# Running one token tile through all layers before the other, with the first tile's expert gather beside the second tile's layers

## The chip, the cores and the metric

The kernel runs on one core of a Trainium2 chip. The metric is the device time of one execution in microseconds, as the median of several runs. All data are float32.

## What is computed

The input `x` has 256 tokens of 1024 channels. Two layers (depth 2) of a mixed block come first, then one block of another kind, then a final RMS norm. Cut to what matters:

```
for l in range(2):                       # layers 0 and 1
    h = x @ w_in[l]                      # 1024 -> 6048, split into ten parts
    y_hg  = hgrn2(q, f, i)               # gated recurrence, 8 heads, causal
    y_mla = latent attention, 8 heads, causal
    y_mem = attention of every token over 256 memory tokens (mem @ w_k, mem @ w_v)
    y = concat(y_hg*silu(g), y_mla*silu(g), y_mem*silu(g)) @ w_out[l]
    x = layernorm(alpha * x + y)
mod = silu(c) @ w_ada + b_ada            # 6 rows of 1024: shifts, scales, gates
h = rmsnorm(x) * (1 + sc1) + sh1
x = x + g1 * (concat(dilated causal attention(h), causal pooling(h)) @ w_out_2)
h2 = rmsnorm(x) * (1 + sc2) + sh2
# experts: 8 heads; per head the top 16 of 128 + 128 sub-keys, then the top 16 of 256 sums
x = x + g2 * sum over 8 heads * 16 picks of  gate * gelu(u[e] . h2) * v[e]
out = rmsnorm(x)
```

Every token picks 128 of 16384 experts. An expert is a row of 2048 numbers (u and v side by side, 8 KB). A token depends on earlier tokens only (and on the memory tokens), never on later ones.

## The kernel before, in words

The tokens stand in two tiles of 128 (`TT = 2`). In layers 0 and 1 every product takes both tiles at once: `channel_major` (L671) multiplies a 128x128 block of weights with 256 token columns, `token_major` (L686) and `output_product` (L707) take 512 weight columns against 128 tokens. Weights are streamed once, as 48 units of mostly 2 MB, into a ring of three slots; SP's queue issues them (`weights`, L497) when the unit three places earlier has been used. The 24 pieces of `w_ada` (1 MB each) go into one buffer, are multiplied by silu(c) on GpSimd (L596 to L599), and are summed over partitions by TensorE in the tasks `AD`.

The order of work on each engine is written out by hand: `PE_ORDER`, `ACT_ORDER`, `DVE_ORDER` for the two layers and a last list each for the third block (L58 to L83). An engine takes its tasks in exactly this order and waits on semaphores where a task's input isn't there. `L01` to `L18` are the levels of the recurrence (products L811, blend L1631), `S`, `P`, `Y` the three steps of an attention batch, `HO`, `HN` the readout and its norm, `LN` the LayerNorm. In the third block `Xt`/`Xu`, `Zt`/`Zu` turn the first and second tile, `K0` to `K3` are the products of the expert queries (L965), `E` the scores against the sub-keys (L975), `R` the search for the top 16 (`route`), `XP` the expert numbers (`experts_of`, L1797 to L1817), `GT` the gates.

The gather begins when the first head's expert numbers are there. GpSimd issues one indirect DMA per pick (L632): partition p receives the row of token p's expert, 128 rows of 8 KB, 1 MB in all. 15 buffers of the earlier layers, freed one by one, take turns as slots (`NEW_SLOTS`, `PICK`). For each pick DVE forms the dot of the row's first half with h2 (L1847), ScalarE takes Gelu and gate (L1313, L1315) and scales an identity matrix by it (L1321), and TensorE multiplies this 128x128 diagonal with the row's second half, 512 columns at a time, into two PSUM banks over 128 picks (L1095). Then the slot may be filled again. First come all 128 picks of the first tile, then those of the second.

## Time and profile before

| | |
|---|---|
| median of 3 runs | 1444.62 us (1444.59 to 1448.75) |
| the profiled execution | 1450.41 us, span 1448.6 us |
| TensorE busy (matmuls) | 1296.5 us, 89% |
| weight loads of TensorE | 803.2 us, 55% |
| DVE busy | 814.1 us, 56% |
| ScalarE busy | 412.2 us, 28% |
| GpSimd busy | 643.4 us, 44% |
| DMA | 407.78 MB, mean 281 GB/s |

The span is the time from the first to the last instruction of the profiled execution. Busy times are for the whole span and average over stages with different limits; matmul ends are modelled, and matmuls overlap in the array, so the time from one start to the next tells more than a mean duration. Each float32 matmul of the program shows as two records. In the lists of waits the name after the arrow is what the engine waited for last.

### The profile page before, as it was taken

To read this page: it belongs to the slowest core of one execution; us is meant where nothing else is said; L and a number is where in the kernel's file an instruction comes from. 1 tells how busy PE (TensorE), PEld (TensorE's weight loads), DVE (VectorE), ACT (ScalarE), POOL (GpSimd) and SP (SyncE) were. 2 spreads that over 40 slices of the span, in tenths; PEclk is the share of its full clock that TensorE was granted. 3 is DMA by queue.
4 is the path that set the end of the run, shared out by engine and by line. 5 is a ranking of instruction groups with operands and counts; after the bars stand their busy time and mean duration, and the time that the engine had idled before them with its cause. 6 is when DMAs were issued, how large, how long until landed. Compare 5 with 4: busy or idle time off the path is not lost.

```text
span 1448.6 us, 16824 instructions
## 1 busy us (share of the span) xinstructions
PE 1296.5 (89%) x5960; PEld 803.2 (55%) x5960; DVE 814.1 (56%) x1681; ACT 412.2 (28%) x1032; POOL 643.4 (44%) x643
## 2 busy tenths in 40 slices
PE   9999999999999999999998989967977787777786
PEld 8877686547877686548656546523333333333332
DVE  0776277331566287432238765789797554544455
ACT  0532333201333333211223332322313232122123
POOL 0556667422546666513102544454544454444450
PEclk9999999999999999999998999988988899999999
DMA  9544234444444344445355999999999999999994
GB/s 374 190 161 175 117 155 186 161 175 175 180 161 175 117 174 188 171 167 200 132 217 209 407 420 392 420 420 419 421 419 420 420 420 420 421 420 420 420 420 203
DMA packets 53597, 407.78 MB, mean 281 GB/s; under 512 B 6133, under 2 KB 8586, under 8 KB 10890
## 3 DMA queue, kind: packets, MB, share of 16 engines
q0 software_dynamic: 36864, 268.45, 45.0%
q1 hardware_dynamic: 15562, 137.21, 24.2%
q10 hardware_dynamic: 1088, 1.05, 0.4%
q8 instruction: 47, 0.77, 0.2%
q14 instruction: 36, 0.29, 0.1%
HBM read 404.56 MB, written 1.07 MB: 280 GB/s over the span
## 4 chain that ended last, share of the span: by engine, by line
PE 29%; DMA 24%; DVE 7%; issue 4%; POOL 3%; ACT 2%; ACTq 0%; POOLq 0%; DVEq 0%
DMA ring<-in_peer_uv,vM 12%; PE bank L1095 9%; PE pj L671 6%; PE pj L707 6%; DMA yT<-in_peer_uv,vM 5%; PE pj L686 3%; DMA qvE<-in_peer_uv,vM 3%; PE pj L965 2%; DMA hv<-in_peer_uv,vM 2%; DMA more_rows<-in_peer_uv,vM 1%; DMA qM<-in_peer_uv,vM 1%; POOL more_rows L598 1%; DVE tri L1847 1%; POOL mod_part L599 1%; DVE big L1847 1%
## 5 line engine op out<-in xcount | busy, mean ns | idle before, releaser
L671 PE MATMUL pj<-xT,ring 128*128 128x256 f32 (+2 forms) x1536 | 326.5, 373 | 2.2 <-ACTq L1143 1.7
L671 PEld LDWEIGHTS pj<-xT,ring 128*128 128x128 f32 (+1 forms) x1536 | 279.3, 190 | 43.2 <-issue 3.6
L598 POOL TENSOR_SCALAR more_rows<-more_rows,lbt 128x256 f32<-128x256 f32 x168 | 172.0, 1024 | 16.4
L632 POOL DMA_INDIRECT ring<-in_peer_uv,vM x101 | 121.5, 1203 | 125.8 <-PE bank L1095 115.0
L596 POOL TENSOR_SCALAR mod_part<-more_rows,lbt 128x256 f32<-128x256 f32 x24 | 26.3, 1096 | 265.5 <-issue 122.0
L707 PE MATMUL pj<-ring,yT 128*128 128x512 f32 x320 | 141.9, 600 | 0.0
L599 POOL TENSOR_TENSOR mod_part<-mod_part,more_rows 128x256 f32<-128x256 f32 x168 | 128.0, 762 | 14.0
L1313 ACT ACTIVATE rope<-vM 128x4 f32<-128x4 f32 (+3 forms) x84 | 17.1, 204 | 408.5 <-DVE big L1847 326.1
L1095 PE MATMUL bank<-ring,tri 128*128 128x512 f32 x204 | 101.4, 638 | 20.9 <-ACT tri L1321 20.9
L1095 PE MATMUL bank<-ring,causal 128*128 128x512 f32 x200 | 99.6, 637 | 19.5 <-ACT causal L1321 19.5
L707 PEld LDWEIGHTS pj<-ring,yT 128*128 128x128 f32 x320 | 60.7, 193 | 72.0 <-issue 72.0
L1847 DVE SCALAR_TENSOR_TENSOR big<-ring,memT 128x1024 f32<-128x1024 f32 x51 | 62.9, 1233 | 48.9 <-DMA ring<-in_peer_uv,vM 48.7
L1847 DVE SCALAR_TENSOR_TENSOR tri<-ring,memT 128x1024 f32<-128x1024 f32 x50 | 61.2, 1224 | 48.6 <-DMA ring<-in_peer_uv,vM 48.5
L1095 PEld LDWEIGHTS bank<-ring,tri 128*128 128x128 f32 x204 | 41.3, 206 | 76.4 <-issue 48.9
L1095 PEld LDWEIGHTS bank<-ring,causal 128*128 128x128 f32 x200 | 39.6, 203 | 72.9 <-issue 45.5
L632 POOL DMA_INDIRECT more_rows<-in_peer_uv,vM x20 | 22.6, 1128 | 122.5 <-DVE vM L1817 79.4
L686 PE MATMUL pj<-ring,xT 128*128 128x512 f32 x160 | 70.5, 595 | 0.0
L1315 ACT ACTIVATE rope<-rope,rstd 128x1 f32<-128x1 f32 x256 | 56.6, 284 | 2.8
L1631 DVE COPY_PREDICATED tri<-level_mask,bank 128x512 f32<-128x512 uint8 x56 | 41.0, 731 | 16.9 <-PE bank L811 14.4
L632 POOL DMA_INDIRECT yT<-in_peer_uv,vM x28 | 31.4, 1121 | 41.0 <-PE bank L1095 39.2
L686 PEld LDWEIGHTS pj<-ring,xT 128*128 128x128 f32 x160 | 29.8, 190 | 34.7 <-issue 34.4
L965 PEld LDWEIGHTS pj<-xT,ring 128*128 128x128 f32 x320 | 44.1, 202 | 5.8 <-issue 4.3
(368 smaller groups left out, 2124.3 us busy)
## 6 DMA issues: line engine op xcount, KB each, us to landing
ring<-in_units SPq DMA_DIRECT2D x44, 2048.0 KB, 9.5
more_rows<-in_w_ada SPq DMA_DIRECT2D x24, 1024.0 KB, 4.8
ring<-in_units SPq DMA_DIRECT2D x2, 1536.0 KB, 6.3
ring<-in_peer_uv,vM POOLq DMA_INDIRECT x101, 23.3
memT<-in_mem SPq DMA_DIRECT2D x1, 1024.0 KB, 5.2
ring<-in_units SPq DMA_DIRECT2D x2, 512.0 KB, 6.6
ring<-in_units SPq DMA_DIRECT2D x1, 1024.0 KB, 9.1
xT<-in_x_turned SPq DMA_DIRECT2D x1, 1024.0 KB, 10.8
```

The lines of the kernel that those rows point to most:

```text
L596: do(g.tensor_scalar(part, mod_w[:, 0, :], silu_c[:, 0:1], None, ALU.mult))
L598: do(g.tensor_scalar(mod_w[:, c, :], mod_w[:, c, :], silu_c[:, c:c + 1], None, ALU.mult))
L599: do(g.tensor_tensor(part, part, mod_w[:, c, :], ALU.add), "mod_partial" if c == DC - 1 else None)
L632: pool.indirect_dma_start(row_slot[k], None, d["peer_uv_2"], bass.IndirectOffsetOnAxis(ap=expert[:, t, j:j + 1], axis=0))\
L671: ins = nc.tensor.matmul(pj[s][0:n, 2 * m + first:2 * m + stop], ring[:, slot, at:at + n], act[:, c, first:stop], start=(c == 0), stop=(c ...
L686: ins = nc.tensor.matmul(pj[s][:, t * COLS:(t + 1) * COLS], act[:, c, t * P:(t + 1) * P], w[:, c, :], start=(c == 0), stop=(c == DC - 1))
L707: ins = nc.tensor.matmul(pj[t][:, n * 512:(n + 1) * 512], yT[:, 4 * j + c, t * P:(t + 1) * P], w[:, c, n * 512:(n + 1) * 512], start=(firs ...
L965: ins = nc.tensor.matmul(pj[s][:, 2 * m * P + first:2 * m * P + stop], w[c][:, m * P:(m + 1) * P], xT[:, c, first:stop], start=(c == 0), s ...
L1095: ins = nc.tensor.matmul(bank[2 * (1 - t) + half][:, :], diag[n % N_DIAG], row_slot[PICK[n][0]][:, c0:c0 + COLS], start=(j == 0), stop=(j ...
L1315: a.activation(weights_of[:, n0 + k:n0 + k + 1], acts[:, n0 + k:n0 + k + 1], ACT.Copy, scale=gate[:, t, j + k:j + k + 1]).then_inc(sem("ro ...
L1631: do(v.copy_predicated(dst, mask, B), *bank_free(key))
L1847: v.scalar_tensor_tensor(out=junk[0 if one else n % 2], in0=row_slot[k][:, 0:D_MODEL], scalar=1.0, in1=normed[:, t, :], op0=ALU.mult, op1= ...
```

## The change

The work is done one tile at a time: stages (layer, tile) in the order (0,0), (1,0), (2,0), (0,1), (1,1), (2,1). The parts:

- Every product of the layers now has 128 token columns (or 128 tokens against 256 weight columns in `token_major`). The weights are cut into pieces of 1 MB (half a unit) in a ring of three 1 MB slots, and each piece is loaded once per tile: 184 loads, 96 for the first tile (8 of them for the memory keys and values, made only once) and 88 for the second.
- What the second tile needs of the first (keys, values, the recurrence's values and cross decays, memory keys and values) is stored to DRAM from each layer and loaded back before the second tile's same layer (`ST`, `LS`: five parts, 2.9 MB per layer each way). For the third block the first tile's keys, values and pooling input stay in SBUF (`kvu`).
- The pooling's running sums on GpSimd become products with window matrices (`MX`) on TensorE.
- The four engines' orders, SP's too, are one list each over all stages. In them the first tile's routing and picks (`D`, `W`: dots, weights and sums of one pair) stand between the second tile's tasks: W0 to W8 before the second tile's first output product, W9 to W33 before that of layer 1, W63 at the end of its expert queries.
- Modulation weights have a ring of four buffers instead of one; all 24 pieces are done within the first tile's stages.
- The first tile's gather has six slots of its own (`slots`), a seventh from pick 64 and an eighth from pick 107; the second tile's gets six more.
- Picks come in pairs. One indirect DMA still moves 128 rows: those of 64 tokens for two picks. h2 is kept in a matching arrangement (`HR`), four copies per part lay out expert numbers and gates (`paired`), and the scaled diagonal has 128 rows and 64 columns (`twice` is the identity folded in two). A pair takes four matmuls with 64 output partitions and 512 columns, as against four with 128 output partitions for two picks before.
- A dot is written in place over the row's first half.

The core of the diff:

```diff
+STAGES = [(0, 0), (1, 0), (2, 0), (0, 1), (1, 1), (2, 1)]
+RING, MOD_RING, FIRST_SLOTS = 3, 4, 6
+AFTER_ROUTING = (0, 1)
+NEW_SLOTS = {0: [0, 1, 2, 3, 4, 5], 64: [6], 107: [10], 136: [7, 8, 9, 11], 140: [12], 167: [13]}
...
-    for n in range(ROWS):
+    for n in range(TT * PICKS):
         if n in NEW_SLOTS:
-            free = list(NEW_SLOTS[n][1]) + free
+            free = list(NEW_SLOTS[n]) + free
         k = free.pop(0)
         out.append((k, last.get(k), sum(1 for q in out if q[0] == k)))
         last[k] = n
-        free.append(k)
+        if n % 2:
+            free += [out[n - 1][0], k]
     return out
...
+        state = [nc.dram_tensor(f"state{l}", (P, 5 * D_MODEL + COLS), f32).ap() for l in range(DEPTH)]
+
+        def state_parts(l):
+
+            y = state[l]
+            return ((kM[:, :, 0:P], y[:, 0:D_MODEL].rearrange("p (h t) -> p h t", t=P)),
+                    (hv[:, 0, :], y[:, D_MODEL:2 * D_MODEL]), (wide(cross[:, :, :]), y[:, 2 * D_MODEL:3 * D_MODEL]),
+                    (kvE[:, :, :].rearrange("p a n -> p (a n)"), y[:, 3 * D_MODEL:5 * D_MODEL]),
+                    (vM[:, 0, :], y[:, 5 * D_MODEL:5 * D_MODEL + COLS]))
 
...
+            def piece(n):
+
+                token = LOADS[n]
                 if n >= RING:
-                    sp.wait_ge(sem("unit_done"), n - RING + 1)
-                slot, first, width = n % RING, 0, UP_W if STREAM[n][1] == "UP" else DC * COLS
+                    old = LOADS[n - RING]
+                    task = old[3:]
+                    if task == "UQ":
+                        bank_filled(sp, old + ":1")
+                    elif task == "UK":
+                        bank_filled(sp, old[:3] + "UV")
+                    elif task[0] == "O":
+                        after(sp, "out_done", old)
+                    elif task[2:] == "a":
+                        after(sp, "half_done", old)
+                    else:
...
+                elif task == "ST":
+
+                    for k in ("I0", "I1", "J0", "J1", "J2", "J3"):
+                        after(sp, k + "_ready", s + k)
+                    after(sp, "uk_ready", s + "UK")
+                    after(sp, "uv_ready", s + "UV")
+                    sp.wait_ge(sem("kr_spread"), 32 * COUNT["kr_sent"][s + "Cr"])
+                    after(sp, "lvl_ready", s + "Db8")
+                    for held, kept in state_parts(l):
+                        sp.dma_start(kept, held).then_inc(sem(f"state_store{l}"), 16)
+                elif task == "LS":
+
+                    for k in range(DEPTH):
+                        sp.wait_ge(sem(f"state_store{k}"), 16 * STATE)
+                    done = "01." if l else "10."
+                    for k in (f"S{batches(1 if l else 0) - 1}", f"Y{batches(1 if l else 0) - 1}", "R1"):
+                        bank_filled(sp, done + k)
+                    for held, kept in state_parts(l):
+                        load(held, kept, "state_load")
+                elif task == "SB":
+
...
+            starts = {t * PICKS + first * TOPK: f"2{t}.XP{part}" for t in range(TT) for part, (first, last) in enumerate(EXPERT_PARTS)}
+            for n in range(TT * PICKS):
+                t, q, c = n // PICKS, n % PICKS // 2, n % 2
+                k, earlier, _ = PICK[n]
                 if n in starts:
-                    pool.wait_ge(sem("experts"), starts[n])
-                if previous is not None:
-                    pool.wait_ge(sem("rows_used"), previous + 1)
...
+                if n == 0:
+                    bank_filled(pool, "MT")
+                    pool.wait_ge(sem("mod_store"), 16)
+                    unit_done(pool, "10.J3")
+                if earlier is not None:
+                    pool.wait_ge(sem("rows_used"), earlier // 2 + 1)
+                elif k == KM_SLOT:
+                    bank_filled(pool, f"11.S{n_mla(1) - 1}")
+                elif RING_SLOT <= k < QK_SLOT:
+                    unit_done(pool, "21.H3")
+                elif k == QK_SLOT:
+                    bank_filled(pool, "21.S3")
+                    after(pool, "sm_ready", "21.S3")
+                elif k == QK_SLOT + 1:
+                    unit_done(pool, "21.H3")
+                elif k == QK_SLOT + 2:
+                    bank_filled(pool, "21.E3")
+                elif k == QK_SLOT + 3:
+                    after(pool, "routed", "21.RT7")
                 pool.indirect_dma_start(row_slot[k], None, d["peer_uv_2"],
-                                        bass.IndirectOffsetOnAxis(ap=expert[:, t, j:j + 1], axis=0))\
+                                        bass.IndirectOffsetOnAxis(ap=expert[t][:, q, c:c + 1], axis=0))\
                     .then_inc(sem(f"row_load{k}"), 16)
...
+                    elif token[0] == "W":
+                        p = int(token[1:])
+                        tile, q = p // PAIRS, p % PAIRS
+                        sums = acc if tile == 0 else pj
+                        if q == 0:
+                            if tile == 0:
+                                pe.wait_ge(sem("acc_free"), EARLY_USES)
+                            else:
+                                for s in range(2):
+                                    pe.wait_ge(sem(f"pj_free{s}"), WIDE_USES[s])
+                        pe.wait_ge(sem("diag_ready"), 2 * p + 2)
                         for half in range(2):
-                            c0 = D_MODEL + half * COLS
-                            ins = nc.tensor.matmul(bank[2 * (1 - t) + half][:, :], diag[n % N_DIAG],
-                                                   row_slot[PICK[n][0]][:, c0:c0 + COLS],
-                                                   start=(j == 0), stop=(j == PICKS - 1))
-                            if j == PICKS - 1 and half == 0:
+                            for c in range(2):
+                                n = 2 * p + c
+                                c0 = D_MODEL + half * COLS
+                                ins = nc.tensor.matmul(sums[64 * c:64 * c + 64, half * COLS:(half + 1) * COLS],
+                                                       diag[:, n % N_DIAG, :], row_slot[PICK[n][0]][:, c0:c0 + COLS],
+                                                       start=(q == 0), stop=(q == PAIRS - 1))
+                            if q == PAIRS - 1 and half == 0:
                                 last(ins, "half_summed")
                         last(ins, "rows_used")
...
+            def expert_weights(p):
+
+                tile, q = p // PAIRS, p % PAIRS
+                part = next(n for n, (a0, a1) in enumerate(EXPERT_PARTS) if a0 <= 2 * q // TOPK < a1)
+                after(act, "gate_ready", f"2{tile}.GT{part}")
+                act.wait_ge(sem("dot_done"), 2 * p + 2)
+                do(a.activation(acts[tile][:, q, :], dots[tile][:, q, :], ACT.Gelu))
+                for c in range(2):
+                    a.activation(weights_of[tile][:, q, c:c + 1], acts[tile][:, q, c:c + 1], ACT.Copy,
+                                 scale=gate[tile][:, q, c:c + 1]).then_inc(sem("row_weight"), 1)
+                if 2 * p >= N_DIAG:
+                    act.wait_ge(sem("rows_used"), p - N_DIAG // 2 + 1)
+                for c in range(2):
+                    act.wait_ge(sem("row_weight"), 2 * p + c + 1)
+                    a.activation(diag[:, (2 * p + c) % N_DIAG, :], twice[:, :], ACT.Copy, scale=weights_of[tile][:, q, c:c + 1])\
+                        .then_inc(sem("diag_ready"), 1)
...
+            def paired(dst, src, first, end, signal=None):
+
+                q0, q1 = first * TOPK // 2, end * TOPK // 2
+                for c in range(2):
+                    for a0 in range(2):
+                        done = c == a0 == 1
+                        do(v.tensor_copy(dst[64 * a0:64 * a0 + 64, q0:q1, c], src[64 * c:64 * c + 64, a0:(end - first) * TOPK:2]),
+                           *((signal,) if done and signal else ()), **({} if done else {"behind": 1}))
...
+                        p = int(token[1:])
+                        tile, q = p // PAIRS, p % PAIRS
+                        if q == 0:
+                            after(dve, "h2_ready", f"2{tile}.HR")
+                        for c in range(2):
+                            k, _, use = PICK[2 * p + c]
+                            dve.wait_ge(sem(f"row_load{k}"), 16 * (use + 1))
+                            row = row_slot[k][:, 0:D_MODEL]
+                            v.scalar_tensor_tensor(out=row, in0=row, scalar=1.0, in1=h2_of[tile][:, c, :], op0=ALU.mult, op1=ALU.mult,
+                                                   accum_out=dots[tile][:, q, c:c + 1]).then_inc(sem("dot_done"), 1)
...
+                elif task == "HR":
+                    bank_filled(dve, s + "Z:1")
+                    if t:
+                        bank_filled(dve, f"11.Y{batches(1) - 1}")
+                    do(v.tensor_tensor(normed, normed, row_scale2, ALU.mult))
+                    do(v.tensor_tensor(h2_of[t][0:64, 0, :], normed[0:64, :], row_shift2[0:64, :], ALU.add))
+                    do(v.tensor_tensor(h2_of[t][64:P, 1, :], normed[64:P, :], row_shift2[64:P, :], ALU.add), "h2_own")
```

## Rows read from the trace of the kernel before

**Rows 1.** The page: 40 equal slices of the span, and the gather's queue.
```profile
GB/s 374 190 161 175 117 155 186 161 175 175 180 161 175 117 174 188 171 167 200 132 217 209 407 420 392 420 420 419 421 419 420 420 420 420 421 420 420 420 420 203
...
q0 software_dynamic: 36864, 268.45, 45.0%
```

**Rows 2.** Windows: us, busy time by engine (instructions), TensorE clock, DMA share, GB/s.
```profile
0.00:741.00 741.00, 719.92 (x4403) 523.38 (x4404) 360.07 (x591) 216.78 (x354) 342.41 (x387) 0.99 0.47 180
...
741.00:850.00 109.00, 97.41 (x465) 65.59 (x464) 75.54 (x229) 35.84 (x99) 36.74 (x30) 0.94 0.72 289
...
850.00:1436.00 586.00, 475.18 (x1089) 212.91 (x1087) 371.41 (x849) 155.18 (x569) 264.19 (x227) 0.92 1.00 413
...
1436.00:1448.60 12.60, 3.97 (x8) 1.35 (x8) 7.10 (x14) 4.45 (x12) 0.00 (x0) 0.80 0.11 42
```

**Rows 3.** Timeline, 760 to 772 us: first head's routing, its expert numbers, first gather.
```profile
762.59 0.49 DVE L1760 MAX8 cT<-sm 128x8 f32<-128x128 f32 x2 [6.92 <-ACTq L1421]
...
767.23 0.18 DVE L1797 CAST cT<-kE 128x32 f32<-128x32 uint32 x1
...
770.19 0.17 DVE L1817 CAST vM<-vM 128x16 uint32<-128x16 f32 x1
...
771.29 1.17 POOL L632 DMA_INDIRECT more_rows<-in_peer_uv,vM  x1 [79.39 <-DVE vM L1817]
```

**Rows 4.** Chain of waits in order of time: start us, us, what, records.
```profile
502.11 20.83 PE pj L671 x96
...
546.54 13.93 PE pj L686 x32
...
757.25 3.59 PE pj L965 x32
...
871.19 6.87 PE bank L1095 x16
```

**Rows 5.** Groups by line and form, TensorE: the memory products.
```profile
L671 PE MATMUL pj<-memT,ring 128*128 128x256 f32 x128 | 28.2, 380 | 0.2 <-DMA ring<-in_units 0.2
...
L686 PE MATMUL pj<-ring,memT 128*128 128x512 f32 x64 | 27.8, 592 | 0.0
```

**Rows 6.** Timeline, DVE, from LayerNorm's scaling to the last block's turned rows.
```profile
654.26 1.28 DVE L1734 SCALAR_TENSOR_TENSOR pT<-x,stat,big 128x1024 f32<-128x1024 f32 x1
...
663.42 1.75 DVE L1550 TENSOR_SCALAR xT<-bank,modc 128x128 f32<-128x128 f32 x4 [2.03 <-PE bank L644]
```

**Rows 7.** Groups by line, GpSimd: the modulation's products and sums.
```profile
L598 POOL TENSOR_SCALAR more_rows<-more_rows,lbt 128x256 f32<-128x256 f32 x168 | 172.0, 1024 | 16.4
...
L599 POOL TENSOR_TENSOR mod_part<-mod_part,more_rows 128x256 f32<-128x256 f32 x168 | 128.0, 762 | 14.0
```

**Rows 8.** Groups by line, DVE: blend, level step, dot.
```profile
L1631 DVE COPY_PREDICATED tri<-level_mask,bank 128x512 f32<-128x512 uint8 x56 | 41.0, 731 | 16.9 <-PE bank L811 14.4
...
L1602 DVE TENSOR_TENSOR big<-b 128x512 f32<-128x512 f32 x28 | 25.6, 916 | 1.0
...
L1847 DVE SCALAR_TENSOR_TENSOR tri<-ring,memT 128x1024 f32<-128x1024 f32 x50 | 61.2, 1224 | 48.6 <-DMA ring<-in_peer_uv,vM 48.5
```

**Rows 9.** Groups by line, ScalarE: table loads at the Gelu.
```profile
L1313 ACT ACT_TABLE_LOAD x8 | 10.3, 1283 | 20.0 <-DVE big L1847 11.2 <-DVE tri L1847 8.6 <-ACT yT L1394 0.2
```

**Rows 10.** Timeline, TensorE: attention values in 64 columns, and the product after them.
```profile
105.80 0.66 PE L791 MATMUL bank<-pT,vM 128*64 128x128 f32 x8
...
106.39 0.92 PE L671 MATMUL pj<-xT,ring 128*128 128x256 f32 x3
```

**Rows 11.** The page's DMA issues: count, KB each, median us to landing.
```profile
ring<-in_units SPq DMA_DIRECT2D x44, 2048.0 KB, 9.5
...
more_rows<-in_w_ada SPq DMA_DIRECT2D x24, 1024.0 KB, 4.8
```

**Rows 12.** DMA issues, 800 to 850 us.
```profile
ring<-in_units SPq DMA_DIRECT2D x1, 2048.0 KB, 12.0
```

**Rows 13.** DMA issues, 850 to 900 us.
```profile
ring<-in_peer_uv,vM POOLq DMA_INDIRECT x8, 9.5
```

2668 lines of the change are left out of this document (1278 added, 1390 removed).

## The prediction

> **What bounds the kernel now.** I read the windows first, then the chain of waits, then the DMA rows. The kernel has two halves with different limits. Up to 741 us TensorE is busy 720 us while the DMA engines move only 180 GB/s; from 850 to 1436 us the DMA share is 1.00 at 413 GB/s and no engine is full [rows 1, 2]. The second half is the gather: 268.45 MB on the software queue [rows 1], 256 indirect loads of 1.05 MB, 128 for each token tile. The first is issued at 771.3 us, because the first expert numbers are ready only at 770.4 us [rows 3]. The slices hold 420 GB/s, so a picked row costs 2.5 us; 12.6 us of finish follow the last landing [rows 2]. So the time is: TensorE time to the first expert, plus bytes after it over 420 GB/s, plus the finish. The profiled execution took 1450.4 us for its span of 1448.6, and is 5.8 us above the median of 1444.6.
>
> **The part before the first gather.** The change halves the tokens of each product. Does a narrow product cost half? Matmuls are recorded twice each; 96 records with 256 columns took 20.8 us (217 ns), 32 with 128 columns 3.6 us (112 ns), 32 and 16 with 512 columns 13.9 and 6.9 us (435, 429 ns) [rows 4]. Cost goes by columns, so nothing is lost. Of the 720 us, the memory products take 27.5 each for the two forms (128 records at 215 ns, 64 at 430) [rows 5]; they are made once, for the first tile. Modulation products are some 11 us, the warm-up 6. (720-55-11-6)/2 = 324, and with memory and modulation 390 us of TensorE until the first tile's middle norm.
>
> Stalls come on top. (a) The start: TensorE's first task now waits for 14 small loads (13 us, estimate from the issue order), and the fifth weight piece is queued behind 6 MB of other loads (11 us at 420 GB/s). (b) With no other tile to fill it, the step from last layer to last block stands bare: LayerNorm, norm and turn took 654.3 to 665.2 us [rows 6]: 11 us. (c) Readout and its norm at each layer's end: about 8 us a layer by DVE's chain of seven 0.7 us steps, less what attention fills, 16 together; attention of the last block 2. (d) The middle norm to the queries, 6 us. That puts the first query product at 451. Three half units of queries (3.45 us each), the scores and their copy take 12; one head's routing took 4.6 us and its expert numbers 3.2 [rows 3], plus four copies that lay out the pairs (0.8). First gather at **472 us** instead of 771. GpSimd's modulation chain (24 pieces of eight 1.02 and seven 0.76 us steps, 13.6 us each) [rows 7] ends near 395 and stays just beside it; the end of the first tile's second layer waits for it if it slips.
>
> **The part after it.** Bytes still to move: gather 268.4; the second tile's 88 weight pieces of 1.05 MB, 92.3; state loads 5.8; LayerNorm rows, biases, windows and modulation rows 6.6; less three pieces already fetched: 370 MB, or 881 us at 420 GB/s. That would end at 1353 if DMA never paused. It pauses:
> - DVE routes eight heads of the first tile (37 us), forms expert numbers and gates (36) and does the second tile's gate arithmetic, seven levels and seven blends (copy 0.73 us, level steps 0.7 to 0.9) [rows 8], 52 with norms, and two pairs of dots (1.22 us each, plus accumulator) [rows 8]: some 131 us, from 463 to 597. Until then only two pairs are used, and six slots hold six rows. In these 125 us DMA has 41 MB to do, 97 us: **28 lost**.
> - From there to the first output product: DVE 46 us, TensorE 29, nine pairs; 47 MB or so against 53 us, 6 lost. ScalarE changes tables between Gelu and Exp for almost every pair; a load took 1.28 us [rows 9], two per pair, so ScalarE too is near full here: 8 lost.
> - The output stretch (8 pieces, 9 pairs, 27 MB, 64 us) against TensorE's 43: DMA bound, none lost. The same holds for the next: 12 pieces and 8 pairs, 70 us against 57; later 8 and 12, 80 against 50; 12 and 13, 95 against 76.
> - Levels and attention of the second layer (14 pieces, 8 pairs, 75 us) hold DVE for 80 and TensorE for 87: 10 lost.
> - The second tile's own routing: first row 30 us after its middle norm, when the first tile's rows run out: 10 lost; then 5 while few slots are free.
> Sum 67. 1353 + 67 + 12.6 = 1433 us span, 1434 for a profiled execution, less 5.8: **1429 us**.
>
> What I cost at nothing: the pairs need the same bytes and two dots of the same width; their sums use 64 columns of the array each. Eight records of 64 columns in alternate halves took 0.59 us until the next product began (105.80 to 106.39) [rows 10], against 0.86 for eight full ones, so halves overlap, and a pair costs 1.72 us instead of 3.43; bound below by that row, above by 3.43. I take 1.72, by the alternating order, though its columns are four times fewer. State stores fall into the first part, where DMA has a third to spare. A weight piece under the gather shares the DMA engines: the one 2 MB unit loaded so took 12.0 us [rows 12], against 9.5 as median of all [rows 11]; 6 us per MB is under the 7.5 us that piece and pair together need of DMA in most stretches. Ring: three slots of 1 MB, two ahead of 3.45 us of products each, so 6.9 us for a landing of some 4.8 us [rows 11]; the cover goes where another load comes between.
>
> Waits that are new on queues: SP must wait for the layer's last levels, memory values and key rows before it stores state, and for the last scores, values and readout of the layer before until it loads it back; the weight pieces stand behind both on SP's queue, and TensorE waits for those. A state load of 2.9 MB is 7 us of DMA, of which the ring covers two; up to 5 us, and only the first of the two falls where TensorE is the bound. I leave it to the range. GpSimd has nothing behind its gather waits but the gather itself. In TensorE's queue each pair's sum stands between weight pieces: a late row holds up the second tile's layers, and a late layer step holds up the slots.
>
> The rule that speaks against more bytes is in the Trainium skill, DMA: Bandwidth & Descriptors, section Where 436 GB/s comes from: between HBM and SBUF it names about 358 GB/s per core as what binds. By that figure 370 MB would take 1033 us and the sum would be about 1585. The trace disagrees: 413 over 586 us [rows 2].
>
> **Rivals.**
> 1. *Slots come back late* (slower). Engines take their tasks in a written order; each pair passes DVE, ScalarE, TensorE, GpSimd, and each of them may stand waiting in the other tile's layers. From 597 us to the second tile's routing 61 pairs pass in 480 us, 7.9 us each. The gather gets slower than before from 8.2 us on; 8.6 gives 1470, 9.0 gives 1490. For it: six slots are three pairs, landing took 9.5 us with about that many slots [rows 13], and dots, weights, sum and reissue of a pair some 9 by their durations, so 6 to 7 us per pair even unhindered. Against: only small gaps between that and the bound of DMA in the dense stretches.
> 2. *Halves of the array do not overlap for long rows* (about the same or slower). TensorE gets 55 us more under the second tile; DMA's slack hides half: +28, 1457. Rows 10 speak against it.
> 3. *Packed as well as before* (faster). Before, TensorE idled only 21 us up to 741 [rows 2]. With as few stalls in the first part the gather starts at 437, and with half the pauses the end is 1429-35-30: 1364.
> 4. *First part or table loads 10 to 20 us worse than summed*: 1440 to 1449, no difference that counts.
> 5. *DMA stops at a lower rate than 420 GB/s* when weight loads and gather mix: at 358 the sum is 1585. 413 over 586 us [rows 2] excludes it for the gather, and the slice from 797 to 833 us, in which a unit was loaded, still ran at 407 [rows 1]; I set no chance aside. The section named above is the source of the figure.
>
> **How the numbers follow.** Forecast as summed, 1400 to 1440: 0.47. Rival 3: 0.11. Rival 4: 0.12. Rival 2: 0.06. Rival 1: 0.24. A difference of 0.3% (4.3 us) is what a measurement of this kernel can tell from none. Faster 0.58, same 0.12, slower 0.30. The likeliest case's own range is 1400 to 1440; the range for all is 1385 to 1475: it takes in the 20 us on either side of the first gather's start, and rival 1 up to 8.7 us a pair.
>
> **What would show it.** In the profile after: first indirect DMA of the first tile near 472 us (right: 455 to 490). Total bytes near 515 MB. A hollow in the DMA share from 490 to 597, then 0.9 or more until about 1075. Records of 64 columns by 512 starting in pairs, 1.7 us for a pair's eight. From the second tile's first row on, as before: 2.5 us per row. DVE nearly full from 465 to 597. Wrong if the DMA share between 600 and 1075 stays under 0.85 (rival 1), if TensorE needs 3.4 us per pair (rival 2), or if the gather starts before 445 or after 500.

## The result, and the profile after

The changed kernel takes **1498.9 us** (median of 4 runs, 1495.1 to 1505.8), the kernel before, measured beside it, 1446.0: ratio 1.0365, 95% interval 1.034 to 1.039. Measured again later, with 5 runs: 1501.5 us, 1.0366 (1.0342 to 1.039). The forecast was 1429 us, range 1385 to 1475: wrong in sign, and outside its range. The profiled execution took 1495.3 us for a span of 1493.5, against the 1433 of the sum.

The page of the changed kernel: the slices' DMA rows, the totals and the two large queues, to lay beside [rows 1].

```profile
span 1493.5 us, 21020 instructions
PE 1166.1 (78%) x7870; PEld 792.0 (53%) x7870; DVE 831.0 (56%) x1836; ACT 503.6 (34%) x1187; POOL 598.0 (40%) x620
DMA  8887777988675986589999888997999999999996
GB/s 324 311 324 285 297 315 280 373 325 316 243 261 216 406 341 249 178 309 386 373 384 421 327 332 337 420 420 313 399 422 370 422 421 393 418 421 422 421 422 263
DMA packets 82575, 517.38 MB, mean 346 GB/s; under 512 B 8853, under 2 KB 17066, under 8 KB 22442
q0 software_dynamic: 36864, 268.45, 44.1%
q1 hardware_dynamic: 43434, 246.53, 43.1%
```

The bytes are as forecast (517.4 MB against 515). What is new is the middle: slices of 178 to 249 GB/s around 600 us, and notches at 327 to 337 and at 313. The windows give the stretches (us, busy time by engine with instructions, TensorE clock, DMA share, GB/s), to lay beside [rows 2]:

```profile
0.00:485.00 485.00, 438.18 (x3445) 373.68 (x3446) 208.37 (x387) 133.77 (x229) 320.30 (x364) 0.95 0.79 297
485.00:540.00 55.00, 49.12 (x399) 45.51 (x398) 42.34 (x182) 16.19 (x29) 9.85 (x10) 0.97 1.00 410
540.00:670.00 130.00, 106.44 (x1038) 84.72 (x1038) 110.84 (x259) 65.99 (x123) 13.02 (x13) 0.93 0.69 248
670.00:840.00 170.00, 132.11 (x913) 82.50 (x912) 80.12 (x141) 56.44 (x128) 41.23 (x38) 0.91 0.97 391
840.00:930.00 90.00, 79.71 (x642) 59.26 (x640) 59.59 (x98) 56.25 (x108) 14.56 (x15) 0.96 0.83 319
930.00:1010.00 80.00, 49.38 (x137) 15.75 (x136) 32.71 (x60) 22.51 (x63) 21.51 (x20) 0.84 1.01 418
1010.00:1030.00 20.00, 15.16 (x91) 9.33 (x92) 5.23 (x9) 5.73 (x20) 6.52 (x6) 0.80 0.60 217
1030.00:1151.00 121.00, 103.31 (x564) 66.74 (x564) 65.84 (x142) 45.77 (x129) 27.82 (x27) 0.93 0.99 405
1151.00:1480.00 329.00, 188.93 (x646) 53.83 (x644) 218.84 (x551) 96.22 (x347) 143.18 (x128) 0.79 1.00 413
```

From the first gather to 1480 us, 372.6 MB move (the stretches' rates times their lengths): 887 us at 420 GB/s in 995 us. So 108 us are **pauses** of the DMA engines, each stretch's length times one less its rate over 420: 1 up to 540, 53 from 540 to 670, 12 up to 840, 22 up to 930, 0, 10 (1010 to 1030), 4, and 6 at the end. The same account of the kernel before, from 771.3 us on (its 407.78 MB less what [rows 2] and the window from 741 to 771.3 us, at 70 GB/s, have outside): 272 MB, 647 us of 665, so some 17 us of pauses. The whole change, in spans: start 286 us earlier, bytes 240 us more, pauses 91 more, finish 1 more: +45. The rates are rounded, so each of these is good to a microsecond or two.

The gather's issues on GpSimd (timeline; in brackets the idle time before it and what ended it):

```profile
485.03 1.16 POOL L716 DMA_INDIRECT slots<-in_peer_uv,chosen  x1 [69.02 <-DVE chosen L1541]
...
527.23 0.94 POOL L716 DMA_INDIRECT slots<-in_peer_uv,chosen  x1 [11.11 <-PE acc L852]
...
629.55 0.94 POOL L716 DMA_INDIRECT slots<-in_peer_uv,chosen  x1 [100.14 <-PE acc L852]
...
1151.38 0.95 POOL L716 DMA_INDIRECT slots<-in_peer_uv,chosen  x1 [24.84 <-DVE chosen L1541]
```

Ten rows (rows are counted from 0) go out in 43 us, then none for 100: the slots wait for the third pair's sum, which stands after the scores of the second tile's first layer in TensorE's order. From row 10 to row 127 the pairs pass at 496 us over 58.5, **8.5 us each**. The waits of 630 to 1151 us (total, times, longest):

```profile
POOL slots L716 <- PE acc L852: 416.0, 49, 100.1
ACT chosen L1132 <- DVE slots L1625: 174.1, 29, 15.2
DVE slots L1625 <- DMA slots<-in_peer_uv,chosen: 154.2, 60, 11.2
...
PE acc L852 <- ACT diag L1140: 54.9, 17, 7.8
...
PEld bank L728 <- DMA sq<-in_peer_subkeys: 20.3, 1, 20.3
PEld pj L801 <- DMA ring<-in_pieces: 19.3, 1, 19.3
PE pj L801 <- DMA ring<-in_pieces: 18.4, 1, 18.4
PE bank L728 <- DMA sq<-in_peer_subkeys: 18.6, 1, 18.6
```

GpSimd waits for TensorE, VectorE for DMA, ScalarE for VectorE's dots, TensorE for ScalarE's diagonals: a ring in which each is late for another. The last four rows are two single waits (weight load and product show both): one for the subkeys, and before it in time one for a weight piece. The latter is seen on SP's queue (timeline, start and length), and in the landings of the state load (660 to 700 us; KB, median us from issue to landing):

```profile
670.42 0.38 SPq L553 DMA_DIRECT2D kM<-state  x1
...
675.00 2.38 SPq L553 DMA_DIRECT2D kvE<-state  x1
677.42 1.66 SPq L553 DMA_DIRECT2D vM<-state  x1
679.12 38.31 SPq L553 DMA_DIRECT2D ring<-in_pieces  x5
```

```profile
kvE<-state SPq DMA_DIRECT2D x1, 1024.0 KB, 17.5
kM<-state SPq DMA_DIRECT2D x1, 512.0 KB, 10.1
...
vM<-state SPq DMA_DIRECT2D x1, 256.0 KB, 25.0
```

A state of 2.9 MB would be 7 us of DMA by itself (estimate at 420 GB/s). Here its last part lands 25 us after its own issue, 32 us after that of the first part (670.4 to 702.4). Up to six gathered rows are in flight beside it, which is the likely reason. The weight piece behind it is late, and TensorE stands from 686.6 to 705.0.

Of the forecast's smaller steps, the halves of the array overlap: between two output products (3.6 us each) the eight records of a pair take 1.94 us; eight with 128 columns took 3.6 to 3.7 (a4).

```profile
670.10 3.60 PE L801 MATMUL pj<-ring,yT 128*128 128x512 f32 x8
673.63 1.94 PE L852 MATMUL acc<-slots,diag 128*64 128x512 f32 x8
675.50 3.70 PE L801 MATMUL pj<-ring,yT 128*128 128x512 f32 x8
```

### The profile page after: what moved, and what is told of

Read it like the earlier page. It is cut to its first block, busy times and chain, and to the rows that moved or that the text cites. A ratio compares the mean times of both kernels' runs of the same rounds, so it can differ in the third digit from the quotient of the medians.

```text
span 1493.5 us, 21020 instructions
## 1 busy us (share of the span) xinstructions
PE 1166.1 (78%) x7870; PEld 792.0 (53%) x7870; DVE 831.0 (56%) x1836; ACT 503.6 (34%) x1187; POOL 598.0 (40%) x620
## 4 chain that ended last, share of the span: by engine, by line
PE 50%; DMA 26%; DVE 13%; ACT 5%; issue 5%; POOL 1%; SPq 1%; ACTq 0%; POOLq 0%; DVEq 0%
PE pj L756 21%; DMA slots<-in_peer_uv,chosen 15%; DMA ring<-in_pieces 6%; PE acc L852 5%; PE pj L767 4%; PE acc L801 4%; PE pj L801 3%; DVE slots L1625 2%; PE pj L779 2%; PE pj L783 2%; DMA qkb<-in_peer_uv,chosen 2%; DMA kM<-cT 2%; DMA sq<-in_peer_subkeys 1%; PE bank L916 1%; PE pj L852 1%
## 5 line engine op out<-in xcount | busy, mean ns | idle before, releaser
L716 POOL DMA_INDIRECT slots<-in_peer_uv,chosen x172 | 185.4, 1078 | 629.1 <-PE acc L852 455.4
L756 PE MATMUL pj<-xT,ring 128*128 128x128 f32 (+1 forms) x3328 | 403.5, 283 | 28.7 <-issue 15.7
L756 PEld LDWEIGHTS pj<-xT,ring 128*128 128x128 f32 (+1 forms) x3328 | 392.2, 197 | 50.2 <-issue 32.6
L1625 DVE SCALAR_TENSOR_TENSOR slots<-slots,apart 128x1024 f32<-128x1024 f32 x116 | 140.6, 1225 | 157.1 <-DMA slots<-in_peer_uv,chosen 154.2
L688 POOL TENSOR_SCALAR slots<-slots,lbt 128x256 f32<-128x256 f32 x168 | 167.8, 999 | 16.4
L852 PE MATMUL acc<-slots,diag 128*64 128x512 f32 x464 | 132.5, 664 | 47.5 <-ACT diag L1140 47.5
L689 POOL TENSOR_TENSOR slots<-slots 128x256 f32<-128x256 f32 x168 | 127.7, 760 | 14.0
L852 PE MATMUL pj<-slots,diag 128*64 128x512 f32 x224 | 83.5, 834 | 59.4 <-ACT diag L1140 59.3
L767 PE MATMUL pj<-ring,xT 128*128 128x256 f32 x384 | 89.8, 388 | 2.9 <-DMA ring<-in_pieces 2.9
L801 PE MATMUL pj<-ring,yT 128*128 128x512 f32 x160 | 76.7, 624 | 19.3 <-DMA ring<-in_pieces 18.4
L767 PEld LDWEIGHTS pj<-ring,xT 128*128 128x128 f32 x384 | 72.3, 193 | 15.1 <-issue 5.2
L1140 ACT ACTIVATE diag<-twice,chosen 128x64 f32<-128x64 f32 x256 | 75.1, 340 | 0.2 <-ACT chosen L1134 0.2
L686 POOL TENSOR_SCALAR slots<-slots,lbt 128x256 f32<-128x256 f32 x24 | 24.6, 1026 | 65.0 <-PE bank L831 36.0
```

What stands on the lines that cost most here:

```text
L688: do(g.tensor_scalar(w[:, c, :], w[:, c, :], silu_c[:, c:c + 1], None, ALU.mult))
L689: do(g.tensor_tensor(part, part, w[:, c, :], ALU.add), "mod_partial" if c == DC - 1 else None)
L716: pool.indirect_dma_start(row_slot[k], None, d["peer_uv_2"], bass.IndirectOffsetOnAxis(ap=expert[t][:, q, c:c + 1], axis=0))\
L756: ins = nc.tensor.matmul(unit_bank(token[:5])[0:n, base + m:base + m + P], w[:, c * 2 * P + m:c * 2 * P + m + n], act[:, c, :], start=(c = ...
L767: ins = nc.tensor.matmul(unit_bank(token[:5])[:, base:base + 2 * P], act[:, c, :], w[:, c * 2 * P:(c + 1) * 2 * P], start=(c == 0), stop=( ...
L801: ins = nc.tensor.matmul(out_bank(l, t)[:, n * COLS:(n + 1) * COLS], yT[:, 4 * j + 2 * half + c, :], w[:, c, n * COLS:(n + 1) * COLS], sta ...
```

## The experiments

Every run is the changed kernel with one edit. "Way" is the time from the first tile's first gather to the second tile's first, by each profile (666 us in the changed kernel, 662 when taken again); it leaves out the start, which moved between 485 and 500 us from one profile to the next. The differences told in the text are of medians; by the ratios, which compare each kernel with the kernel before measured beside it, they come out within 5 us of that (b4: 82 for 86). b1 and b2 have two runs each, the others four to six.

| run | us | ratio to before (95%) | way, us |
|---|---|---|---|
| changed kernel | 1498.9 | 1.0365 (1.034-1.039) | 666 |
| again (e0) | 1501.5 | 1.0366 (1.0342-1.039) | 662 |
| a1 Square for Gelu | 1484.6 | 1.0258 (1.0238-1.0279) | 653 |
| a2 half pieces | 1456.9 | 1.0065 (1.0042-1.0088) | 626 |
| a3 loads spread | 1488.7 | 1.0288 (1.0251-1.0326) | 655 |
| a4 whole rows | 1524.7 | 1.0524 (1.0481-1.0567) | 683 |
| b1 layers alone | 1315.4 | 0.9078 (0.904-0.9115) | 478 |
| b2 rows unused | 1466.4 | 1.012 (1.0083-1.0157) | 626 |
| b3 pairs earlier | 1524.3 | 1.0531 (1.049-1.0572) | 693 |
| b4 four slots | 1585.3 | 1.0933 (1.0895-1.0971) | 744 |
| c1 seventh slot | 1491.6 | 1.0321 (1.0269-1.0372) | 657 |
| c2 sums later | 1550.1 | 1.0704 (1.0654-1.0754) | 719 |
| c3 no state | 1488.2 | 1.0282 (1.0234-1.0331) | 656 |
| d1 half routing | 1497.7 | 1.0326 (1.0292-1.0361) | 655 |
| d2 half products | 1487.9 | 1.0295 (1.0248-1.0341) | 647 |
| e1 d1 and d2 | 1481.0 | 1.0232 (1.0214-1.025) | 639 |
| e2 a1 and a3 | 1479.5 | 1.0211 (1.0189-1.0234) | 645 |
| d3 a1, a3, c1 | 1487.7 | 1.0277 (1.025-1.0304) | 646 |

**What the parts cost.** First the table loads:

```diff
-                do(a.activation(acts[tile][:, q, :], dots[tile][:, q, :], ACT.Gelu))
+                do(a.activation(acts[tile][:, q, :], dots[tile][:, q, :], ACT.Square))
```

> The changed kernel with Gelu of the picks' dots replaced by Square, which needs no table of its own (the activation of the gathered rows is therefore another function; all else is the same). In the changed kernel ScalarE loads a table 103 times, 1.28 us each, 27 of them right before a Gelu and some 30 before the next Exp or Ln. Theory P (written order and pauses: no pair is summed from 527 to 626 us, and pieces stand behind other loads on SP's queue): these loads stand beside idle time of ScalarE and cost 0 to 10 us, so 1489 to 1499. Rival A (ScalarE holds the pairs up in the dense stretches): 57 loads of 1.28 us are 73 us, a third or more of it shows, 1475 or below. Rival B (only bytes count): 1499 within 4 us.

14 us less. Table loads fall from 104 (not 103, as the expectation has it) to 44, 60 of 1.28 us: of 77 us of ScalarE a fifth shows. It lies between theory P and rival A. The forecast had 8 us for them. The Trainium skill, ScalarE: Activation LUTs, section What ACT_TABLE_LOAD costs, gives 1283 ns for the load, as [rows 9] do, and a drain that makes 2.66 us of each switch; where the next activation starts 10 ns after the load, as in this trace, the drain doesn't show behind it.

The changed kernel's timeline shows such a load and the activation behind it:

```profile
501.61 1.28 ACT L1132 ACT_TABLE_LOAD   x1
502.90 0.20 ACT L1132 ACTIVATE chosen<-chosen 128x2 f32<-128x2 f32 x1
```

Then the bytes (only the first half of each second-tile piece is loaded):

```diff
+                elif token[1] == "1":
+                    load(ring[:, n % RING, 0:D_MODEL], d["pieces"][at, :, 0:D_MODEL], f"ring_load{n % RING}")
```

> The changed kernel with only the first half of each weight piece of the second token tile loaded (the products read what the ring held before in the other half, so the second tile's values are others). 88 pieces of 0.52 MB less are 46 MB, some 110 us at 420 GB/s. Rival B (the bytes after the first gather decide): 1390 to 1400. Theory P: the stretches 540-670, 840-930 us, where DMA had a share of 0.69 and 0.83, gain nothing, and from 670 to 840 and 930 to 1151 TensorE (132 of 170, 168 of 221 us busy) and the chain of the pairs come next: 50 to 80 us, 1420 to 1450, and the DMA share between 670 and the second tile's first row falls below 0.9.

42 us less, of 110 us that the 46 MB take at 420 GB/s. That is less than either theory had it (theory P: 50 to 80). The bytes bind for two fifths of what they weigh; take them away, and the way is still 626 us. The expectation's last clause fits too (windows, as above):

```profile
670.00:840.00 170.00, 141.76 (x1013) 89.51 (x1013) 86.51 (x150) 63.85 (x141) 41.38 (x37) 0.90 0.87 334
840.00:1030.00 190.00, 155.38 (x913) 94.44 (x910) 100.16 (x172) 84.12 (x199) 45.92 (x45) 0.90 0.85 331
```

The loads that stand before others on SP's queue:

```diff
-PC PC 01.GB PC 11.LS PC PC PC PC PC PC PC PC ...
+PC PC 01.GB PC PC PC 11.LS PC PC PC 11.LP4 PC PC PC PC 11.LP1 PC PC PC 11.LP2 PC PC PC 11.LP3 ...
-21.MR 21.SB PC PC
+21.SB PC 21.MR PC
```

> The changed kernel with the second state load cut in five, one part after each three or four weight pieces, and the subkeys and block tables of the second tile issued in the order of their use, the modulation rows last. Same bytes. Theory P: TensorE's two waits of 18.4 and 18.6 us for loads (a weight piece behind the state, the subkeys behind 3.4 MB of tables) go, with the 12 and 10 us that DMA stood still around them: 10 to 22 us less, 1477 to 1489. Rival B (only bytes count) or rival C (the pairs' chain catches up on the waits anyway): 1499 within 5 us.

10 us less with the same bytes; the intervals of the two kernels touch no longer. In its trace the wait for the subkeys is gone, and the longest one of an output product for its piece is 7.4 us. And the state itself, stores and loads left out:

> The changed kernel without the stores and loads of the state (the second tile then attends to the wrong first-tile keys, values and states; it is left out of the computation that these are the right layer's). 11.5 MB less, 5.8 of them after the first gather: 14 us at 420 GB/s. Spreading the second load had given 10 us with the same bytes. If only the bytes count: 14 us less, 1485. If the waits behind it count (TensorE 18.4 us for the piece behind the state): 20 to 30 us less, 1469 to 1479. If it is hidden: 1494 or more.

11 us less, where its loads after the first gather alone are 14 us of DMA and spreading them had given most of it. It doesn't tell whether bytes or waits count; it shows that the state costs about 11 us, with its waits. That this gain and that of a3 are not to be added is likely, since both go by the same load; no run has the two together.

The picks in pairs, undone (sums of 128 columns, one pick of all tokens in each row, the layout copies gone):

```diff
-                                ins = nc.tensor.matmul(sums[64 * c:64 * c + 64, half * COLS:(half + 1) * COLS],
+                                ins = nc.tensor.matmul(sums[:, half * COLS:(half + 1) * COLS],
-                    a.activation(diag[:, (2 * p + c) % N_DIAG, :], twice[:, :], ...
+                    a.activation(diag[:, (2 * p + c) % N_DIAG, :], eye[:, :], ...
```

> The changed kernel with the picks in pairs undone: each gather brings one pick of all 128 tokens, the sum uses 128 columns for each row. Bytes, gathers, dots and slots are the same; TensorE needs 3.4 to 3.7 us for two rows instead of 1.94. Between the first tile's first gather and the second tile's last row that is 128 times some 1.6 us. Theory P: under the second tile TensorE is busy 0.8 of the time and in 485-670 us 0.84, so of 61 x 1.6 = 98 us half or more shows, and in the last part nothing (189 + 100 of 329 us): 1540 to 1600. Rival B (only bytes count) : 1499 within 10 us. Rival of my forecast's kind (halves of the array do not overlap) is already excluded by 1.94 us for a pair's eight records.

26 us more; theory P said 41 or more. A pair then takes 3.6 to 3.7 us, and the way grows by 17 to 21 us. TensorE is busy 74 us more on the way, not the 98 expected, and its granted clock is higher, 0.97 for 0.92, so this run changes two things at once (way in the changed kernel, then in a4):

```profile
485.00:1151.00 666.00, 535.23 (x3773) 363.83 (x3773) 396.67 (x887) 268.87 (x598) 134.50 (x128) 0.92 0.89 355
```

```profile
495.00:1178.00 683.00, 609.34 (x3755) 419.54 (x3754) 390.08 (x856) 273.77 (x596) 134.97 (x128) 0.97 0.88 345
```

Pairs pay, by 26 us; the other parts of the change were not undone one by one.

**What holds the way.** Two kernels take the first tile's pairs 1 to 62 apart (cut; the second part of the edit, the small load in place of the gather, is in b1 alone):

```diff
+                            if 0 < p < PAIRS - 1:
+                                dve.sem_inc(sem("dot_done"), 1)
+                                continue
...
+                if 2 <= n < PICKS - 2:
+                    pool.dma_start(row_slot[k][:, 0:64], d["peer_uv_2"][0:P, 0:64]).then_inc(sem(f"row_load{k}"), 16)
+                    continue
```

> The changed kernel with the first tile's pairs 1 to 62 left out: no gather (a load of 32 KB stands in its place), no dot, weight or sum. The first and last pair stay, the second tile is complete. In the changed kernel the second tile's first row is issued 666 us after the first tile's; TensorE is busy 534 us of them, some 125 with the pairs. Theory P (the pairs' work and their waits in TensorE's and VectorE's written order take what the layers leave): the layers alone take 534 - 125 = 409 us and 60 us of their own stalls, so the second row's start falls from 1151 to 950-980 us, the time to 1300-1330. Rival C (the layers of one tile alone, with nothing to fill their dependences, are the long chain): it stays above 1050, the time above 1400.

> As before, but the gathers stay with all their bytes, and only the dots, weights and sums of pairs 1 to 62 are left out; a slot is still given back at its pair's place in the written order. The 666 us hold 237 MB, 565 us at 420 GB/s. Theory P: the engines' work goes (dots 152 us of VectorE, sums 125 of TensorE), the bytes bind where they can: the second tile's first row at 1060 to 1100 instead of 1151, the time 1410 to 1450. Rival D (weight pieces land late because the gather shares the DMA engines, and that holds TensorE): above 1120, the time above 1470. Rival E (the engines' work was all of it): as without gathers, below 1000.

Without gathers and pairs the way is 478 us, as theory P had it. With the gathers, but no work of an engine on them, it is 626; with that work, 662 to 666. So of the 188 us that the first tile's picks add to the second tile's layers, 148 come from rows that must land and slots that are given back at their places in the order, and only 40 from dots, weights and sums. More than half of the 148 is plain bytes: b2 moves 236 MB on its way (377 GB/s), 562 us at 420 GB/s, so the way can't be shorter than that; the other 64 us are pauses. The split is not quite clean, since the granted clock on the way is 0.85 in b2 and 0.93 in b1, and TensorE is busy 428 and 408 us there. The time, 1466, lies above theory P's 1450 and just below rival D's 1470; D's mechanism is in the waits of this kernel, where nothing else is in TensorE's way (490 to 1160 us):

```profile
PE bank L728 <- DMA sq<-in_peer_subkeys: 43.5, 1, 43.5
...
PE pj L801 <- DMA ring<-in_pieces: 33.9, 5, 25.9
```

With the queue of rows always full, the subkeys keep TensorE 43.5 us and one piece 25.9. Rival E is out.

**The places and the slots.** Fewer slots, one more, and other places:

```diff
-NEW_SLOTS = {0: [0, 1, 2, 3, 4, 5], 64: [6], 107: [10], 136: [7, 8, 9, 11], 140: [12], 167: [13]}
+NEW_SLOTS = {0: [0, 1, 2, 3], 64: [6], 107: [10], 136: [4, 5, 7, 8, 9, 11], 140: [12], 167: [13]}
```

> The changed kernel with four slots instead of six for the first tile's rows (until the second tile's fifth pair). Rival 1 of the forecast in its narrow form (a slot's way round, landing, dots, weights, sum, reissue, is the bound): a pair's way of some 9 to 12 us now has two pairs in flight instead of three, so up to 1.5 times the 5.5 us of dense stretches: 60 us or more, 1560 or above. Theory P (places in the written order are the bound, slots only bridge the pauses of up to 25 us): two rows less are 5 us of DMA at each of the some ten pauses, 20 to 50 us: 1519 to 1549. If slots never count: 1499 within 5 us.

86 us more, as rival 1 in its narrow form said, and far beyond theory P's 50. Two pairs in flight leave VectorE waiting for rows (630 to 1240 us), against 154.2 in the changed kernel:

```profile
DVE slots L1625 <- DMA slots<-in_peer_uv,chosen: 257.9, 71, 20.6
```

The seventh slot (8 KB made of the first tile's x and xT, side by side; its last residual is lost):

> The changed kernel with a seventh slot for the first tile's rows 6 to 121: the 8 KB of the first tile's x and xT (so the first tile's last residual is lost; nothing else is left out). Two slots fewer had cost 86 us. Theory S (a slot's way round is too long for six slots, rival 1 of the forecast): 15 to 35 us less, 1465 to 1485. If six slots are just enough and only fewer hurt: 1494 to 1504.

7 us less, and the interval overlaps that of the changed kernel: at most a small gain. Below six slots the way round binds; a seventh brings little, so at six it is something else that holds most of the time. Then each sum one task later in TensorE's order (cut; the last two lines are where the subkeys are turned, `21.SK`):

```diff
-01.UK 01.UV 01.N0 01.S0 01.S1 W2 01.R1 01.P0 W3 01.S2 01.N1 01.Y0 01.P1 01.S3 W4 W5 01.Y1 01.P2 01.S4 01.P3 W6
+01.L7 01.L8 01.R0 01.UK 01.UV 01.N0 01.S0 01.S1 01.R1 W2 01.P0 01.S2 W3 01.N1 01.Y0 01.P1 01.S3 01.Y1 W4 W5
...
-11.O3b W41 W42 W43 21.SK W44 21.X W45 21.B0a W46 21.B0b 21.B1a W47 21.B1b 21.B2a 21.S0 W48 21.B2b 21.S1 21.B3a
...
+W37 11.O2b W38 11.O3a W39 11.O3b W40 21.SK W41 W42 W43 21.X W44 21.B0a W45 21.B0b W46 21.B1a 21.B1b W47 21.B2a
```

> The changed kernel with each pair's sum of the first tile one task later in TensorE's order (most often one weight piece of 3.65 us or one attention step). TensorE waited 55 us for diagonals between 630 and 1151 us, 17 times, and ran at 1.2 GHz after most of them. Theory W (these waits are what holds the second tile's layers): 15 to 30 us less, 1469 to 1484. Theory S (slots come back too late as it is): every slot comes back 1 to 4 us later, 10 to 40 us more, 1509 to 1539.

51 us more, beyond theory S's range. The 55 us in which TensorE waits for diagonals were not the loss that they look like: in this kernel they are 15.1 us, yet the slots come back later, and the rest waits longer (waits of 630 to 1217 us):

```profile
DVE slots L1626 <- DMA slots<-in_peer_uv,chosen: 228.0, 68, 22.2
...
PE bank L729 <- DMA sq<-in_peer_subkeys: 31.4, 1, 31.4
```

Part of the 51 us comes from one place: the new order puts the turning of the subkeys (`21.SK`) before the sums W41 to W43, so the slots of these three pairs now come back behind that wait for a load, which is 31.4 us for 18.6. Some 13 of the 51 us are therefore likely this one place, not the delay of each sum. The expectation says that TensorE ran at 1.2 GHz after most of its waits for diagonals; of the 17 in the changed kernel's trace, nine were followed by a pair of 1.94 us and eight by one of 2.8 to 3.7 us. And six pairs moved up, to where none is summed for 100 us (the seventh and eighth slot come at rows 76 and 117 instead of 64 and 107, which keeps their places in the layers; cut):

```diff
-01.Q1b 01.F1a 01.F1b W1 01.Q0a 01.Q0b 01.G0a 01.G0b 01.G1a 01.G1b 01.C0a 01.C0b 01.Cn 01.G2a 01.L1 01.G2b 01.G3a
+01.F0b 01.Q1a W0 01.Q1b 01.F1a 01.F1b W1 01.Q0a 01.Q0b W2 01.G0a 01.G0b W3 01.G1a 01.G1b 01.C0a 01.C0b 01.Cn
+W4 01.G2a 01.L1 01.G2b 01.G3a W5 01.G3b 01.M0a 01.M0b W6 01.L2 01.Cr 01.I0a 01.I0b W7 01.L3 01.L4 01.I1a 01.L5
```

> The changed kernel with six more pairs of the first tile placed in the first layer of the second, between 530 and 626 us, where none was summed for 100 us and DMA had a share of 0.7; the six places taken out are near the second tile's middle norm. The other places keep their distance. Same work. Theory P (pauses of DMA there are paid in full): 12 rows are 12.6 MB, 30 us of DMA; VectorE and TensorE, busy 0.85 and 0.82 in this stretch, take 15 and 12 us more there and as much less at the end: 10 to 20 us gained, 1479 to 1489. Rival F (TensorE and VectorE are the bound up to 626 us and the DMA pause is only their shadow): no gain, 1494 to 1504.

Neither theory holds: 25 us more. The row of index 24 is issued at 677 us as before, though six pairs have passed earlier, so the layer has fallen behind by six pairs. The timeline of TensorE in this kernel shows how:

```profile
573.66 3.68 PE L854 MATMUL acc<-slots,diag 128*64 128x512 f32 x8 [3.88 <-ACT diag L1142]
577.27 3.97 PE L758 MATMUL pj<-xT,ring 128*128 128x128 f32 x32
581.17 0.76 PE L918 MATMUL bank<-big 128*32 128x32 f32 x64
...
596.74 3.68 PE L854 MATMUL acc<-slots,diag 128*64 128x512 f32 x8 [7.46 <-ACT diag L1142]
```

The level product L918 (01.L1) stands behind the sum W4, and W4 behind a diagonal that ScalarE makes after other work; VectorE then waits 12.7 us for that level. Four pairs put into this stretch of dependent steps (W4 to W7) cost 19.6 us of TensorE's waiting for diagonals, beside their own sums. This shows that these places were bad ones, not that every place there is.

**The first stretch.** Half the routing away, half the products away, and both:

```diff
+                if t == 0 and e >= 4:
+                    dve.sem_inc(sem("routed"), 1)
+                    return
...
+                    chunks = DC // 2 if token[:3] == "01." else DC
```

> The changed kernel without the routing of the first tile's heads 4 to 7: their expert numbers and gates are copies of those of heads 0 to 3 (the gather's bytes, dots and sums stay). Some 35 us of VectorE's work between 485 and 626 us go (four routings of 4.6 us, two sets of expert numbers and gates). If VectorE (0.85 busy there) is what sets the place of the second pair's sum at 626 us: 20 to 35 us less, 1464 to 1479. If TensorE or the written order does: 0 to 8 us less, 1491 to 1499.

> The changed kernel with the second tile's first-layer products summed over four of eight blocks of the model dimension (24 pieces, half of 3.65 us each: 44 us of TensorE; the pieces are still loaded whole). If TensorE (0.82 busy from 540 to 670 us) sets the place of the second pair's sum: 30 to 44 us less, 1455 to 1469. If VectorE does: 0 to 8 us less. If the two take turns in waiting for each other: 10 to 25 us less for this one and for the run before.

> Half the routing and half the first layer's products of the second tile left out at once (the edits of d1 and d2 together). Alone they gave 1 and 11 us. Theory TB (from 485 to 628 us TensorE, 126 of 143 us busy, and VectorE, 120 of 143, are both the bound, so that either alone keeps the stretch): from the first gather to the sum of the third pair (row 10's issue) 105 to 120 us instead of 145, and 25 to 40 us less in all, 1459 to 1474. If dependences (level by level) or the written order hold it with idle engines: 12 us less, as the sum of the two, 1483 to 1491.

From the first gather to row 10's, in the order changed kernel, d1, d2, e1 (one window of each profile):

```profile
485.00:630.00 145.00, 128.16 (x1288) 115.86 (x1287) 121.91 (x385) 52.05 (x82) 10.30 (x11) 0.96 0.78 296
```

```profile
499.00:638.00 139.00, 125.81 (x1287) 113.81 (x1286) 90.30 (x237) 51.62 (x81) 10.15 (x11) 0.98 0.80 308
```

```profile
494.00:631.00 137.00, 95.95 (x932) 82.66 (x931) 119.77 (x382) 49.69 (x77) 9.87 (x10) 0.89 0.81 314
```

```profile
500.00:628.00 128.00, 95.31 (x936) 80.99 (x935) 90.34 (x240) 51.00 (x78) 9.86 (x10) 0.85 0.87 336
```

Take 32 us from VectorE and 6 go; 32 from TensorE and 8 go; both, and 17 go, with TensorE busy 95 and VectorE 90 of 128 us. So it isn't one engine, and not two full ones alone either: e1 saves a little more than the sum, but less than theory TB's 25 to 40, and its stretch is 128 us where TB said 105 to 120. By elimination, what is left of this stretch is the dependence from step to step of the first layer (level by level between the three engines) in its written order; no run shows that directly. With less to do TensorE also ran at a lower granted clock (0.89 in d2, 0.85 in e1, for 0.96), so the halved products gave back less than their work. Of the times, d1's 1497.7 can't be told from none, d2's is 11 to 14 us less (its interval just touches that of the changed kernel), e1's 18 to 21.

**Do the gains add up?** Three reliefs at once, and two:

> Three reliefs at once on the changed kernel: the loads spread (10 us alone), Square for Gelu (14 us alone), the seventh slot (7 us alone, the first tile's last residual lost). If each pause is paid for itself: 31 us less, 1468. If they overlap: 1475 to 1485. If they help each other (a pause can be bridged only when both ends are free): 1450 to 1465. To beat the kernel before, 1445 is needed.

> The loads spread and Square for Gelu, without the seventh slot. Alone 10 and 14 us; with the seventh slot, three together gave 11. If the reliefs overlap since each only moves the wait to the next thing in the written order: 1480 to 1488. If the seventh slot spoilt the sum: 1470 to 1478.

> The changed kernel itself once more, in the same call as the next two, so that differences of some 10 us can be read against it. Every theory: 1499 within 5 us, ratio to before 1.034 to 1.039.

The loads spread and Square together give 22 us against the changed kernel measured beside them, near the sum of 24; the seventh slot added to them takes 8 back. Why it does stays open. With the two the kernel is still 33 us behind the one before. Of all runs only b1 is faster than that, and it leaves out the first tile's picks.

## Why the prediction was wrong, point by point

The forecast put the first gather at 472 and the end of the span at 1433; the profile has 485 and 1493.5. The step that failed is the count of the pauses between the two tiles' first gathers: load waits on the weights' queue were left at nothing or up to 5 us, and slots that come back late had no term. The 60.5 us are 13 (start) + 6 (bytes: 887 us at 420 GB/s, not 881) + 41 (pauses: 108, not 67) + 1 (finish: 13.5, not 12.6); the other 9 us up to the medians are where each profiled execution stands to its median (5.8 above it forecast, 3.6 below it found).

- **What bounds the kernel**: right, and it holds after the change: 420 GB/s wherever the share is 1.00. Rival 5 is out, weights and gather mixed run at 418 from 930 to 1010 us, where the section Where 436 GB/s comes from of the Trainium skill's DMA: Bandwidth & Descriptors would let 358 bind.
- **The part before the first gather**: the first query product started at 461.0 instead of 451 (the terms as listed add up to 449), and from there 24 us passed instead of 21. "Cost goes by columns, so nothing is lost" is nearly right at the same clock: 64 records with 128 columns took 7.31 us, half of 13.98 is 6.99, which is 8 us over the 1521 of this part. And the clock isn't the same. It was 0.95 up to 485 us, and 0.93 up to 497 in the second profile, against 0.99 up to 741 in [rows 2]. TensorE was busy 438 us where the steps sum to 390 and at most the 21 that follow; 0.04 of 438 is 17 of these 27. GpSimd's chain ended at 415, not 395, and was still no bound.
- **463 to 597, "DVE full"**: a wrong description. The stretch from the first gather to the third pair's sum took 145 us, not 125, with TensorE busy 128 and VectorE 122; I had added up VectorE alone. d1, d2 and e1 show that neither engine's sum gives the length. The pauses there and up to the first output product are 54 us, not 42. (In the next step's "47 MB or so" the unit must be us: nine pairs are 19 MB, 45 us.) Even so, the length of the two stretches together came out as forecast, 185 us (485 to 670) for 186. That is luck: 20 us too few in one and too many in the other. The 64 us by which the way exceeds its forecast (666 for 602) all arise behind 670: 18 more, 3 less, 22 more, 15 more (in order of time) in the four stretches below, and 13 more in the last one (130 us, 1021 to 1151, for some 117).
- **The output stretches**: 82 us (670 to 752), not 64, and 95 (926 to 1021), not 80. Here the step failed most plainly: "up to 5 us" for a state load, left to the range, measured 18.4 us of TensorE's time, and the block's tables, for which I had nothing, 18.6. I had divided their bytes by the full rate, though up to six rows of 1 MB were in flight on the same DMA engines. a3 gives back 10 us of it.
- **The layer stretches**: 67 us, not 70, and then 107 (819 to 926), not 85, with 22 us of pauses for 10. Each stretch of levels and attention has few places for pairs: row 60 waited 22.6 us for its slot, and row 65 22.7.
- **Table loads**: 8 us, put down for one stretch; measured 14 to 16 for all of them (a1).
- **The second tile's routing and last part**: 30 us as forecast from its norm, then 342 us to the end for 359. 15 us had been put down for pauses around the first row, of which some 9 came: 3 in the 26 us before it (368 GB/s), 6 after it.
- **Costed at nothing**: the 64-column sums overlap (1.94 us, not 1.72, and 3.4 to 3.7 where the clock had dropped). That the pairs' waits are covered was wrong as a whole: b2 shows 64 us of pauses on the way (626 us for 562 of bytes) with no dot, weight or sum in it.

**Rival 1**, at 0.24, is what happened in kind: 8.5 us per pair, and from 630 us, not 597. By its own figures (8.6 gives 1470, 9.0 gives 1490) that pace alone is 1465, so it too was priced too low. b4 and c2 show the slots' return as the term with the steepest price. Its sign, "the DMA share between 600 and 1075 stays under 0.85", was badly chosen: the share was 0.89. The pace of the pairs and the share differ because the weights fill the share while the pairs wait. Rivals 2, 3 and 4 are out; rival 2's own price, 28 us, is near what a4 measured (26) when the halves were given up.

And the sum itself: its gain was the difference of two large terms: 299 us of start for 234 of bytes as forecast, 286 for 240 as measured. The margin, 65 us and in truth 46, was to pay for all pauses of a plan in which four engines and two queues wait for each other in a fixed order; 67 was a sum of known gaps, with no term for the ring of waits.
